# A mixture of 32 experts whose weights stream from HBM: pairs in a loop with a ring of 12 chunks, against experts unrolled with a ring of 21

## The chip, the cores and the metric

The kernel runs on one core of a Trainium2 chip. The metric is device time in microseconds (us). Five engines work side by side: PE (TensorE, matrix products), DVE (VectorE), ACT (ScalarE), POOL (GpSimd) and SP (SyncE, which here only issues transfers). They meet through semaphores. Sixteen DMA engines bring data from HBM to SBUF, the on-chip memory.

## What is computed

One encoder layer on 256 tokens of width 1024, all float32: a mixer (recurrence, attention, output product), then 32 experts, of which each token uses four, then a last norm. The change is in the experts and the last norm:

```
for e in range(N_EXPERTS):                         # 32
    gu = t @ w_gate_up[e] + b_gate_up[e]           # 1024 x 2048
    gate = minimum(gu[:, :1024], 7); up = clip(gu[:, 1024:], -7, 7)
    glu = gate * sigmoid(1.702 * gate)
    y = ((up + 1) * glu) @ w_down[e] + b_down[e]   # 1024 x 1024
    out = out + combine[:, e:e+1] * y
return rmsnorm(x + out, g_final)
```

## The kernel before

The mixer streams 40 chunks of 1 MB and ends at about 315 us. The experts follow. An expert's weights are 12 chunks of 1,048,576 bytes: eight of `w_gate_up` (a chunk is 128 rows, one row of 8 KB to each partition) and four of `w_down` (256 rows; each partition gets two rows of 4 KB that lie apart, `(i p) n`). All 32 experts are 384 chunks, 402.7 MB.

Only the tokens that chose an expert are worked on, up to 64 of them (`SLOTS`). For two experts at once (a pair) PE gathers their tokens by a product with a 0/1 matrix `sel` (`gather`, 16 matmuls into the PSUM banks `ga` and `gb`); ACT and DVE copy the result to `hg`. For each expert PE then runs `gate_up` (a bias product, then 8 chunks of 4 matmuls into `pj`), DVE and ACT form the activation in `prod`, PE turns it over (four transposes into `ga`), ACT copies it to `actT`, PE runs `down` (4 chunks of 4 matmuls into `gb`), ACT copies the result to `Y`, and PE adds it to the four output sums (`scatter`: 4 matmuls into `acc`, with the weighted selection `selWT`). PE does this in the written order, two experts in the body of a loop (`pair` in `Fori`, 15 passes after a first one written out). The matmuls of an fp32 product show in the trace as two records each, so an expert's `gate_up` is 64 records and its `down` 32.

SP issues one transfer for a chunk. A chunk of the ring of 12 is free when PE has finished the chunk that lay there (`chunk_done`). Before the experts start, 17 chunks are issued: the ring and five further buffers (`extra`) that are used only once. The mixer's `ring[0..7]` are the same bytes. SP's loads for expert 1 begin with chunk 3, since 0, 1, 2, 8 and 9 of it are already in the ring.

At the end DVE adds the residual `x_sb` to the four sums (`y_summed`), ACT squares and sums, and DVE scales and stores in two pieces.

## Time and profile before

| | |
|---|---|
| time, median of 3 runs | 1300.62 us (1297.96 to 1301.53) |
| span of the profiled execution | 1303.5 us |
| PE busy | 1167.4 us, 90% |
| DVE, ACT, POOL busy | 353.4, 265.5, 136.0 us |
| mean granted clock of TensorE | 0.964 |
| read from HBM | 448.19 MB |
| mixer | 0 to about 315 us |
| experts (first gate product to last down product) | 328.9 to 1292.2 us |

No time of the profiled execution is known apart from its span, so the span stands for it; it is 2.9 us above the median. "Busy" of PE counts each matmul from its start to a modelled end, with neighbours overlapping. A DMA share of 1.00 means that all 16 DMA engines had work all the time.

### The profile page before, as it was taken

Reading aid. Unit: us, or ns where it says so; the run is one execution under the profiler, and the core shown is the slowest. Engines: PE = TensorE matmul, PEld = TensorE weight load, DVE = VectorE, ACT = ScalarE, POOL = GpSimd, SP = SyncE. Lnnn points to the kernel's source line nnn. Section 1 sums busy time; section 2 is a strip of 40 time slices with the busy share of each in tenths; the row PEclk is TensorE's granted clock in tenths of the full one; section 3 lists DMA queues with packets and bytes.
Section 4 is the critical chain, followed back from the end, with each engine's and each line's share of the span. In section 5 each row is a group of like instructions: output and inputs, shape, how many; then the busy total and the mean of one; then the engine's idle time right before and its main releaser. Section 6 shows DMA issues by size and latency. Waiting matters only on the chain.

```text
span 1303.5 us, 16385 instructions
## 1 busy us (share of the span) xinstructions
PE 1167.4 (90%) x6418; PEld 613.3 (47%) x6418; DVE 353.4 (27%) x536; ACT 265.5 (20%) x378; POOL 136.0 (10%) x78
## 2 busy tenths in 40 slices
PE   4989999998998989898898989898989889898986
PEld 4988999988333333333333323332333323333322
DVE  5976888553111111111111111111111211111112
ACT  3536556534110101010101011010101010101102
POOL 5333333653000000000000000000000000000000
PEclk8989999998899989999999999999989999899999
DMA  9843444568499999999999999999999999999991
GB/s 251 259 140 122 158 131 146 169 210 352 182 386 417 409 409 410 418 418 418 418 418 415 417 416 417 417 417 418 418 418 418 418 418 418 418 416 417 417 417 48
DMA packets 118082, 449.75 MB, mean 345 GB/s; under 512 B 10416, under 2 KB 51456, under 8 KB 85280
## 3 DMA queue, kind: packets, MB, share of 16 engines
q1 hardware_dynamic: 117328, 447.04, 86.6%
q0 software_dynamic: 720, 2.23, 0.6%
q8 instruction: 24, 0.39, 0.1%
q14 instruction: 10, 0.08, 0.0%
HBM read 448.19 MB, written 1.05 MB: 345 GB/s over the span
## 4 chain that ended last, share of the span: by engine, by line
PE 85%; ACT 6%; DVE 5%; POOL 2%; issue 1%; DMA 1%; SPq 0%; DVEq 0%; ACTq 0%
PE pj L1155 34%; PE gb L1171 19%; PE pj L999 15%; PE s L1180 3%; PE ga L1133 3%; PE gb L1133 2%; PE pt L1180 2%; PE ga L1162 2%; PE pj L1150 2%; ACT mo L575 1%; ACT mo L573 1%; ACT w_hi L454 1%; POOL w_lo L386 1%; DVE GL L899 1%; DVE V L893 1%
## 5 line engine op out<-in xcount | busy, mean ns | idle before, releaser
L1155 PE MATMUL pj<-ring,GL 128*64 128x512 f32 x2024 | 441.3, 594 | 0.0
L1155 PEld LDWEIGHTS pj<-ring,GL 128*64 128x64 f32 x2024 | 142.6, 137 | 282.5 <-issue 282.5
L1171 PE MATMUL gb<-ring,mo 128*64 128x512 f32 x1008 | 242.4, 637 | 21.3 <-ACT mo L573 21.3
L889 DVE TENSOR_SCALAR V<-pj 128x512 f32<-128x512 f32 x32 | 22.1, 692 | 814.8 <-PE pj L1155 814.8
L1171 PEld LDWEIGHTS gb<-ring,mo 128*64 128x64 f32 x1008 | 74.2, 146 | 170.0 <-issue 140.8
L999 PE MATMUL pj<-hT_hi,w_hi 128*128 128x256 f32 x448 | 130.8, 292 | 15.0 <-DVE hT_lo L649 9.2
L386 POOL TENSOR_TENSOR w_lo<-ring,w_hi 128x1024 fp32r<-128x1024 f32 x40 | 113.3, 2833 | 170.3 <-ACT w_hi L454 170.3
L569 ACT ACTIVATE V<-V 128x512 f32<-128x512 f32 x32 | 20.1, 630 | 532.6 <-DVE V L889 532.6
L999 PE MATMUL pj<-hT_lo,w_hi 128*128 128x256 f32 x448 | 128.3, 286 | 0.0
L999 PE MATMUL pj<-hT_hi,w_lo 128*128 128x256 f32 x448 | 128.2, 286 | 0.0
L999 PEld LDWEIGHTS pj<-hT_hi,w_hi 128*128 128x128 f32 x448 | 87.4, 195 | 16.7 <-issue 16.5
L454 ACT ACTIVATE w_hi<-ring 128x2048 fp32r<-128x2048 f32 x40 | 76.4, 1910 | 86.7 <-PE pj L999 80.2
L999 PEld LDWEIGHTS pj<-hT_lo,w_hi 128*128 128x128 f32 x448 | 87.6, 196 | 0.2
L999 PEld LDWEIGHTS pj<-hT_hi,w_lo 128*128 128x128 f32 x448 | 87.5, 195 | 0.0
L644 DVE TENSOR_TENSOR w_lo<-ring,w_hi 128x1024 fp32r<-128x1024 f32 x40 | 66.8, 1669 | 55.1 <-ACT w_hi L454 51.9
L575 ACT ACTIVATE mo<-gb 128x512 f32<-128x512 f32 x32 | 19.1, 597 | 250.6 <-PE gb L1171 250.6
L1162 PE MATMUL ga<-ident,mo 128*128 128x128 f32 x128 | 23.3, 310 | 48.4 <-DVE mo L895 35.9
L1180 PE MATMUL s<-mo,GL 64*128 64x512 f32 x128 | 36.1, 641 | 22.3 <-ACT mo L575 22.3
L1162 PEld LDWEIGHTS ga<-ident,mo 128*128 128x128 f32 x128 | 14.9, 152 | 56.5 <-DVE mo L895 39.4
L1133 PEld LDWEIGHTS ga<-L,h 128*128 128x128 f32 x272 | 33.3, 200 | 14.4 <-issue 13.0
L1133 PE MATMUL ga<-L,h 128*128 128x128 f32 x272 | 36.6, 290 | 1.3 <-DVE L L869 1.3
L1180 PEld LDWEIGHTS s<-mo,GL 64*128 64x128 f32 x128 | 9.6, 184 | 50.5 <-ACT mo L575 50.5
(277 smaller groups left out, 1066.5 us busy)
## 6 DMA issues: line engine op xcount, KB each, us to landing
ring<-in_w_gate_up SPq DMA_DIRECT2D x253, 1024.0 KB, 10.6
ring<-in_w_down SPq DMA_DIRECT2D x126, 1024.0 KB, 9.6
ring<-in_w_in SPq DMA_DIRECT2D x28, 1024.0 KB, 6.3
ring<-in_w_lru_out SPq DMA_DIRECT2D x4, 1024.0 KB, 4.9
ring<-in_w_fox_out SPq DMA_DIRECT2D x4, 1024.0 KB, 5.6
ring<-in_w_o SPq DMA_DIRECT2D x4, 1024.0 KB, 4.9
extra<-in_w_gate_up SPq DMA_DIRECT2D x3, 1024.0 KB, 8.3
extra<-in_w_down SPq DMA_DIRECT2D x2, 1024.0 KB, 6.1
```

What stands on the lines that cost most here:

```text
L386: g.tensor_tensor(w_lo[c % 2][:, KT // 2:, :], src[:, KT // 2:, :], w_hi[c % 2][:, KT // 2:, :].bitcast(F32), ALU.subtract).then_inc(lo_po ...
L454: act.activation(w_hi[c % 2][:, :, :], ring[:, c % MIX_RING, :].rearrange("p (k n) -> p k n", k=KT), ACT.Identity).then_inc(hi_ready, 1)
L575: act.activation(Y, gb[:, :], ACT.Identity).then_inc(y_ready, 1)
L644: v.tensor_tensor(w_lo[c % 2][:, 0:KT // 2, :], src[:, 0:KT // 2, :], w_hi[c % 2][:, 0:KT // 2, :].bitcast(F32), ALU.subtract).then_inc(lo ...
L889: v.tensor_scalar(gate, pj[0][:, :], LIMIT, None, ALU.min).then_inc(gate_ready, 1)
L999: last = mm(pj[b][:, a * S:(a + 1) * S], lhs, rhs, start=(k == 0 and n == 0), stop=(k == KT - 1 and n == 2))
L1133: last = mm((ga, gb)[k // 4][:, k % 4 * P:(k % 4 + 1) * P], h2[:, t, k * P:(k + 1) * P], sel[:, t, :, 0:SLOTS], start=(t == 0), stop=(t == ...
L1150: mm(pj[b][:, :], onehot[:, i, :], bgu[:, b * 512:(b + 1) * 512], start=True, stop=False)
L1155: last = mm(pj[q // 2][h:h + SLOTS, :], hg[:, c, i, :], w[:, q * 512:(q + 1) * 512], start=False, stop=(c == GU_CHUNKS - 1))
L1162: last = nc.tensor.transpose(ga[:, j * P:(j + 1) * P], prod[:, j * P:(j + 1) * P], ident[:, :])
L1171: last = mm(gb[h:h + SLOTS, :], actT[:, f % 4, f // 4, :], w[:, a * D + q * 512:a * D + (q + 1) * 512], start=(f == 0), stop=(f == KT - 1))
L1180: last = mm(acc[t][q][:, :], selWT[h:h + SLOTS, i, t * P:(t + 1) * P], Y[h:h + SLOTS, :], start=False, stop=True, skip_group_check=True)
```

## The change

1. The 32 experts are written out on PE, ACT and DVE, and the 384 loads on SP; the loops are gone.
2. The weights go through 21 buffers (`slot`). The first 19 chunks, in order of use, go to buffers that come free during the mixer and the routing; two more (`LATE_SLOTS`: the bytes of `LG` and `x_sb`) come free when the output sums have been opened (`sums_open`). From chunk 19 on a load waits for the last user of its slot.
3. `w_down` is read as `(p i) n`: a partition gets two neighbouring rows, 8 KB that lie together. The transposes of the activation pick every second column to match.
4. On PE, the gather of the next pair is cut into halves, one behind each expert's `gate_up`; the scatter of expert n-1 stands behind `gate_up` of expert n, half ahead of the transposes of the activation and half behind them. The transposes write `pj` and not `ga`. `y_ready` is waited for an expert later.
5. The residual is added by PE when the sums are opened (four products with the identity, ACT's first sigmoid waits for them). The last norm reads the sums in PSUM: DVE's four additions go, ACT squares from PSUM into `junk` with a wait after each, all four squares before the first root, and DVE scales in four pieces of 512.
6. `sel` is 128x256 and not 128x512; `selW` is built in two operations. `bgu_raw` is loaded after the attention's last product and not after its last scores. `g_final` is loaded when slot 19 has had its last chunk (number 363 of 0 to 383).

The core of the diff (the loop over a pair in the overflow rounds, which these inputs don't enter, is left out):

```diff
-EXTRA = (0, 1, 2, 8, 9)
+FIRST_SLOTS, LATE_SLOTS = 19, 2
+N_SLOTS = FIRST_SLOTS + LATE_SLOTS
+CYCLE = (*range(GU_CHUNKS), *range(FIRST_SLOTS, N_SLOTS), *range(GU_CHUNKS, FIRST_SLOTS))
+SLOT_OF = [*range(FIRST_SLOTS)] + [CYCLE[q % N_SLOTS] for q in range(ALL_CHUNKS - FIRST_SLOTS)]
...
+        slot_at = [k_at, *mix_at[0:5], hl_at, mix_at[5], xc_at, lp_at, mix_at[6], mix_at[7], whi_at[0], wlo_at[0], r_at, i_at,
+                   whi_at[1], wlo_at[1], q_at, lg_at, x_at]
...
-                    src = w_down[bass.ds(e, 1), 2 * j * P:2 * (j + 1) * P, :].rearrange("e (i p) n -> p (e i) n", p=P)
-                    buf = buf.rearrange("p (i n) -> p i n", i=2)
+                    src = w_down[bass.ds(e, 1), 2 * j * P:2 * (j + 1) * P, :].rearrange("e (p i) n -> p (e i n)", i=2)
...
-            with sp.Fori(2, N_EXP) as e:
-                load_expert(e, e * EXP_CHUNKS + MIX_CHUNKS)
+            for q, s in enumerate(SLOT_OF):
+                if USER_BEFORE[q] is None:
+                    free_after[slot_at[s]]()
+                else:
+                    sp.wait_ge(chunk_done, MIX_CHUNKS + USER_BEFORE[q] + 1)
+                load_chunk(q // EXP_CHUNKS, q % EXP_CHUNKS, s)
...
-            g.wait_ge(chunk_done, MIX_CHUNKS + GU_CHUNKS)
+            g.wait_ge(chunk_done, MIX_CHUNKS + LAST_USER[LG_SLOT] + 1)
             g.dma_start(gfin_b, g_final.rearrange("(a n) -> a n", a=1).broadcast_to([P, D])).then_inc(gfin_loaded, 16)
...
+            act.wait_ge(sums_open, 1)
+            for n in range(N_EXP):
+                sigmoid_of(n)
+                if n % 2 and n + 1 < N_EXP:
+                    hg_copy(n // 2 + 1)
+                actT_copy(n)
+                if n % 2 == 0:
+                    if n:
+                        act.wait_ge(scattered, TT * n)
+                    selWT_copy(n // 2)
...
+                Y_copy(n)
...
+            act.wait_ge(gfin_loaded, 16)
             for t in range(TT):
+                act.wait_ge(scattered, TT * N_EXP - 1 + t)
                 for h in range(2):
-                    act.wait_ge(y_summed, 2 * t + h + 1)
-                    act.activation(h2[:, t, h * 512:(h + 1) * 512], yo[:, t, h * 512:(h + 1) * 512], ACT.Square,
+                    act.activation(junk, acc[t][h][:, :], ACT.Square,
                                    accum_out=stat[:, 40 + 2 * t + h:41 + 2 * t + h]).then_inc(sumsq3, 1)
+                    act.wait_ge(sumsq3, 2 * t + h + 1)
...
-            for t in range(TT):
-                dve.wait_ge(scattered, TT * N_EXP - 1 + t)
-                for h in range(2):
-                    v.tensor_tensor(yo[:, t, h * 512:(h + 1) * 512], x_sb[:, t, h * 512:(h + 1) * 512], acc[t][h][:, :],
-                                    ALU.add).then_inc(y_summed, 1)
...
+                        last = mm(acc[t][h][:, :], ident[:, :], x_sb[:, t, h * 512:(h + 1) * 512], start=False, stop=True,
+                                  skip_group_check=True)
+                last.then_inc(sums_open, 1)
...
+            for n in range(N_EXP):
+                p, i = divmod(n, 2)
...
+                gate_up(i, chunk_at)
+                if n == 0:
+                    open_sums()
+                if p + 1 < PAIRS:
+                    if i == 0:
+                        pe.wait_ge(sel_ready, p + 2)
+                    else:
+                        pe.wait_ge(y_ready, n)
+                    gather_half(i)
+                if i == 0:
+                    pe.wait_ge(selw_ready, p + 1)
+                    pe.wait_ge(up_ready, n + 1)
+                    transpose_selW()
+                if n:
+                    pe.wait_ge(y_ready, n)
+                    scatter(1 - i, 0)
+                pe.wait_ge(act_ready, n + 1)
+                transpose_act()
+                if n:
+                    scatter(1 - i, 1)
+                pe.wait_ge(actT_ready, n + 1)
+                if i == 1 and p + 1 < PAIRS:
+                    pe.wait_ge(hgb_ready, p + 2)
+                down(chunk_at)
```

First place, PE in the body of the loop, the first expert of a pair, from the last matmul of `gate_up` to the bias product of the next expert. `ring` holds weights, `PT` is the weighted selection, `mo` holds `prod`, `actT` and `Y`, `GL` holds `hg` and `selWT`:

```order
L1155 MATMUL pj1<-ring_49,GL_67 64x512 x2
L1200 MATMUL gb<-ident,PT 128x128 x4
L1160 REGISTER_ALU
L1162 MATMUL ga<-ident,mo_76 128x128 x4
L1171 MATMUL gb<-ring_49,mo_76 64x512 x8
L1143 REGISTER_ALU
L1171 MATMUL gb<-ring_49,mo_76 64x512 x8
L1180 MATMUL s0<-mo_76,GL_67 128x512
L1180 MATMUL s1<-mo_76,GL_67 128x512
L1180 MATMUL pt<-mo_76,GL_67 128x512
L1180 MATMUL po<-mo_76,GL_67 128x512
L1150 MATMUL pj0<-bgu_78,onehot_80 128x512
```

The same place in the changed kernel (expert 2). `V` holds the activation and `actT`, `Y` has a buffer of its own:

```order
L1166 MATMUL pj1<-slot10_93,GL_74 64x512 x2
L1155 MATMUL ga<-GL_74,h2_82 128x128 x8
L1173 MATMUL pj1<-ident,selW_108 128x128 x4
L1196 MATMUL s0<-Y_107,GL_74 128x512
L1196 MATMUL s1<-Y_107,GL_74 128x512
L1178 MATMUL pj0<-ident,V_73 128x128 x4
L1196 MATMUL pt<-Y_107,GL_74 128x512
L1196 MATMUL po<-Y_107,GL_74 128x512
L1189 MATMUL gb<-slot11_94,V_73 64x512 x4
L1189 MATMUL gb<-slot12_95,V_73 64x512 x4
L1189 MATMUL gb<-slot13_96,V_73 64x512 x4
L1189 MATMUL gb<-slot14_97,V_73 64x512 x4
```

Half a gather (L1155) and two halves of the scatter of the expert before (L1196) now stand around the transposes of the activation (L1178), and nothing stands between `down` and the next bias product.

Second place, SP's loads after the mixer's last chunk in the kernel before:

```order
L285 DMA ring_49<-in_w_gate_up 128x2048 x5
L285 DMA extra2_73<-in_w_gate_up 128x2048
L285 DMA ring_49<-in_w_gate_up 128x2048
L285 DMA extra0_71<-in_w_gate_up 128x2048
L285 DMA extra1_72<-in_w_gate_up 128x2048
L285 DMA ring_49<-in_w_gate_up 128x2048 x2
L285 DMA ring_49<-in_w_down 128x2x1024
L285 DMA extra8_74<-in_w_down 128x2x1024
L285 DMA ring_49<-in_w_down 128x2x1024
L285 DMA extra9_75<-in_w_down 128x2x1024
L285 DMA ring_49<-in_w_down 128x2x1024 x2
L285 DMA ring_49<-in_w_gate_up 128x2048 x5
```

In the changed kernel, from the last chunk that needs no chunk of an expert to be finished (number 18) on:

```order
L301 DMA slot18_101<-in_w_gate_up 128x2048
L301 DMA slot0_83<-in_w_gate_up 128x2048
L301 DMA slot1_84<-in_w_down 128x2048
L301 DMA slot2_85<-in_w_down 128x2048
L301 DMA slot3_86<-in_w_down 128x2048
L301 DMA slot4_87<-in_w_down 128x2048
L301 DMA slot5_88<-in_w_gate_up 128x2048
L301 DMA slot6_89<-in_w_gate_up 128x2048
L301 DMA slot7_90<-in_w_gate_up 128x2048
L301 DMA slot19_102<-in_w_gate_up 128x2048
L301 DMA slot20_103<-in_w_gate_up 128x2048
L301 DMA slot8_91<-in_w_gate_up 128x2048
```

Before, the eighteenth load waits for chunk 3 of expert 0. Now the twentieth (`slot0`) waits for chunk 0 of expert 0, the next seven for chunks 1 to 7, then two for `sums_open`. A load of `w_down` is one run of 2048 numbers to a partition and not two of 1024.

## Rows read from the trace of the kernel before

**Rows 1.** Windows: us, busy PE PEld DVE ACT POOL, granted clock, DMA share, GB/s.
```profile
325.00:337.00 12.00, 11.50 (x62) 5.48 (x63) 1.16 (x4) 2.13 (x3) 0.00 (x0) 0.98 0.05 11
...
352.00:357.00 5.00, 5.00 (x24) 1.64 (x22) 0.00 (x0) 0.00 (x0) 0.00 (x0) 0.93 0.00 2
...
366.00:1272.00 906.00, 816.88 (x3854) 311.19 (x3852) 115.04 (x180) 90.18 (x135) 0.00 (x0) 0.97 1.02 416
```
**Rows 2.** Waits of PE from 340 to 1280: waiter, releaser: us, times, longest.
```profile
PE ga L1162 <- DVE mo L895: 35.9, 15, 2.4
PE s L1180 <- ACT mo L575: 21.6, 31, 0.7
PE gb L1171 <- ACT mo L573: 21.3, 31, 0.7
PE ga L1162 <- DVE GL L899: 11.8, 15, 0.8
```
**Rows 3.** Timeline of SP's queue: start us, us, line, count.
```profile
335.97 7.20 SPq L285 DMA_DIRECT2D ring<-in_w_gate_up  x5
356.60 2.10 SPq L285 DMA_DIRECT2D ring<-in_w_down  x2
```
**Rows 4.** The chain that ended last, in order of time: start us, us.
```profile
328.91 13.88 PE pj L1155 x64
...
633.36 13.91 PE pj L1155 x64
...
652.02 9.34 PE gb L1171 x32
...
694.89 13.91 PE pj L1155 x64
...
753.74 13.91 PE pj L1155 x64
```
**Rows 5.** Timeline, between first and second product: start us, us, [idle before <- releaser].
```profile
708.71 0.66 PE L1200 MATMUL gb<-ident,PT 128*128 128x128 f32 x4
...
711.75 0.66 PE L1162 MATMUL ga<-ident,mo 128*128 128x128 f32 x4 [2.39 <-DVE mo L895]
...
713.10 7.09 PE L1171 MATMUL gb<-ring,mo 128*64 128x512 f32 x32 [0.69 <-ACT mo L573]
...
722.80 0.73 PE L1150 MATMUL pj<-bgu,onehot 128*128 128x512 f32 x2
...
737.34 2.05 PE L1133 MATMUL ga<-L,h 128*128 128x128 f32 x16
```
**Rows 6.** Timeline, opening of the four output sums.
```profile
343.31 1.98 PE L1125 MATMUL s<-LG,L 32*128 32x512 f32 x4
...
346.05 1.91 PE L1125 MATMUL po<-LG,L 32*128 32x512 f32 x2
```
**Rows 7.** Windows inside one pair of experts, columns as in rows 1.
```profile
703.00:719.00 16.00, 12.92 (x64) 4.63 (x62) 3.97 (x6) 1.71 (x3) 0.00 (x0) 1.00 1.01 423
721.00:729.00 8.00, 8.00 (x36) 2.79 (x38) 0.00 (x0) 0.00 (x0) 0.00 (x0) 1.00 1.03 410
```
**Rows 8.** DMA of the page, parts 3 and 6: queues, issues, us to landing.
```profile
q8 instruction: 24, 0.39, 0.1%
...
ring<-in_w_gate_up SPq DMA_DIRECT2D x253, 1024.0 KB, 10.6
```
**Rows 9.** Timeline of the end.
```profile
1292.26 0.60 ACT L575 ACTIVATE mo<-gb 128x512 f32<-128x512 f32 x1 [7.19 <-PE gb L1171]
...
1294.81 0.63 ACT L604 ACTIVATE h<-yo 128x512 f32<-128x512 f32 x1
...
1299.11 1.28 DVE L952 SCALAR_TENSOR_TENSOR yo<-yo,stat,extra 128x1024 f32<-128x1024 f32 x1
```
**Rows 10.** Windows around a clock drop, columns as in rows 1.
```profile
654.00:656.00 2.00, 2.00 (x6) 0.49 (x6) 0.00 (x0) 0.00 (x0) 0.00 (x0) 0.50 1.00 418
656.00:658.00 2.00, 2.00 (x10) 0.66 (x8) 0.00 (x0) 0.00 (x0) 0.00 (x0) 0.87 1.01 422
```

More of the change, by code:

```diff
@@ L195, in hybrid_block @@
         acc = [[ps[0], ps[1]], [pt, po]]
[L198 to L199 removed]
+        mix_loaded = [sem(f"mix{i}_loaded") for i in range(MIX_RING)]
+        loaded = [sem(f"slot{i}_loaded") for i in range(N_SLOTS)]
         x_loaded = [sem(f"x{t}_loaded") for t in range(TT)]
@@ new lines, in open_sums, with gather_half @@
+                        last = mm(acc[t][h][:, :], ident[:, :], x_sb[:, t, h * 512:(h + 1) * 512], start=False, stop=True,
+                                  skip_group_check=True)
+                last.then_inc(sums_open, 1)
+            def gather_half(b):
+                for k in range(b * KT // 2, (b + 1) * KT // 2):
+                    for t in range(TT):
+                        last = mm((ga, gb)[b][:, k % 4 * P:(k % 4 + 1) * P], h2[:, t, k * P:(k + 1) * P], sel[:, t, :, :],
+                                  start=(t == 0), stop=(t == TT - 1))
+                last.then_inc(gathered, 1)
@@ new lines, in gate_up @@
+            def gate_up(i, chunk_at):
+                for b in range(2):
+                    mm(pj[b][:, :], onehot[:, i, :], bgu[:, b * 512:(b + 1) * 512], start=True, stop=False)
+                for c in range(GU_CHUNKS):
+                    w = chunk_at(c)
+                    for q in range(4):
+                        h = SLOTS * (q % 2)
+                        last = mm(pj[q // 2][h:h + SLOTS, :], hg[:, c, i, :], w[:, q * 512:(q + 1) * 512],
+                                  start=False, stop=(c == GU_CHUNKS - 1))
+                    last.then_inc(chunk_done, 1)
@@ L1178, in scatter, with down @@
+            def down(chunk_at):
+                for c in range(DN_CHUNKS):
+                    w = chunk_at(GU_CHUNKS + c)
+                    for a in range(2):
+                        f = 2 * c + a
                         for q in range(2):
                             h = SLOTS * q
-                            last = mm(acc[t][q][:, :], selWT[h:h + SLOTS, i, t * P:(t + 1) * P], Y[h:h + SLOTS, :],
-                                      start=False, stop=True, skip_group_check=True)
-                        last.then_inc(scattered, 1)
@@ L1214, in expert_round, with scatter @@
-                if first:
-                    pair(0, True)
-                with pe.Fori(int(first), PAIRS) as p:
-                    pair(p)
-            expert_round(0, 0, 0, True)
+                            last = mm(gb[h:h + SLOTS, :], actT[:, f % 4, f // 4, :],
+                                      w[:, a * D + q * 512:a * D + (q + 1) * 512], start=(f == 0), stop=(f == KT - 1))
+                    last.then_inc(chunk_done, 1)
+            def scatter(i, t):
+                for q in range(2):
+                    h = SLOTS * q
+                    last = mm(acc[t][q][:, :], selWT[h:h + SLOTS, i, t * P:(t + 1) * P], Y[h:h + SLOTS, :],
+                              start=False, stop=True, skip_group_check=True)
+                last.then_inc(scattered, 1)
@@ L1220, in _, with chunk_at @@
             over = pe.value_load(flag_i[0:1, 0:1], min_val=0, max_val=1)
+            pe.wait_ge(y_ready, N_EXP)
+            for t in range(TT):
+                scatter(1, t)
             with pe.If(over > 0):
                 with pe.Fori(1, ROUNDS) as r:
-                    expert_round(r * (PAIRS + 1), r * N_EXP, r * PAIRS)
+                    with pe.Fori(0, PAIRS) as p:
+                        pair = r * PAIRS + p
+                        pe.wait_ge(sel_ready, pair + 1)
+                        gather_half(0)
+                        gather_half(1)
+                        pe.wait_ge(hga_ready, pair + 1)
+                        pe.wait_ge(hgb_ready, pair + 1)
+                        pe.wait_ge(onehot_ready, pair + 1)
+                        for i in range(2):
+                            n = r * N_EXP + p * 2 + i
+                            def chunk_at(c):
+                                pe.wait_ge(loaded[c], n * 16 + 16 * (SLOT_OF.count(c) - N_EXP + 1))
+                                return slot[c]
+                            gate_up(i, chunk_at)
+                            pe.wait_ge(act_ready, n + 1)
+                            if i == 0:
+                                pe.wait_ge(selw_ready, pair + 1)
+                                transpose_selW()
+                            transpose_act()
+                            pe.wait_ge(actT_ready, n + 1)
+                            pe.wait_ge(selwt_ready, pair + 1)
+                            down(chunk_at)
+                            pe.wait_ge(y_ready, n + 1)
+                            for t in range(TT):
+                                scatter(i, t)
```

439 lines of the change are left out of this document (204 added, 235 removed).

## The prediction

> **What bounds the kernel now.** I read the windows by stage first. From 366 to 1272 us the DMA engines have a share of 1.02 and move 416 GB/s [rows 1]: they never run dry. In the same stretch PE is busy 817 of 906 us, and the list of its waits names no transfer: it waits for DVE's activation (35.9 us in 15 times, once in a pair of experts) and for three kinds of copies (21.6, 21.3 and 11.8 us) [rows 2]. So two things run at almost one pace. PE takes 58.85 us for a pair of experts where the clock holds (694.89 to 753.74), and 61.53 where it drops (633.36 to 694.89, with a `down` of 9.34 us) [rows 4]. The transfers need 24 chunks of 1.0486 MB at 416 GB/s, 60.5 us. Every load waits for a chunk that PE has finished, so PE's clock still sets when loads start; but a PE that is faster alone gains little, since the transfers take over.
>
> The chunks are 384. The windows show two holes ahead of the steady part: 325 to 337 us at 11 GB/s and 352 to 357 us at 2 GB/s [rows 1]. SP's queue says why: the 18th chunk goes out at 335.97, after chunk 3 of expert 0, and behind the five of that burst the next two wait until 356.60 [rows 3]. The full stretch ends at 1272 us [rows 1], while PE's last `down` ends just ahead of ACT's copy at 1292.26 [rows 9]: PE is 20 us behind the transfers.
>
> **PE after the change.** Between the two products of an expert before, the transposes start at 711.75 where the product ended at 708.71, and `down` at 713.10 [rows 5]. Of this 4.39 us, 0.66 are the `selW` transposes, 0.66 those of the activation, 2.39 and 0.69 are idle. Now half a gather (2.05, from 737.34 [rows 5]), the `selW` transposes (0.66) and half a scatter (1.0: from the end of `down` at 720.19 to the bias product at 722.80 [rows 5] are 2.6 us, 0.7 of them idle [rows 2]) stand in the 3.04 us until the activation is ready: 3.7 us of work, no wait left. For the second expert it is 2.05 + 1.0 = 3.05 us, just enough. The other half of the scatter covers the 0.69 us of ACT's copy, and `Y` is wanted an expert later, so the 0.7 us ahead of each scatter go too. Idle time in a pair is 35.9/15 + 11.8/15 + 2 x 21.6/31 + 2 x 21.3/31 = 5.9 us [rows 2]. PE's own work is then 58.85 - 5.9 = 53.0 us a pair, 26.5 an expert.
>
> The transfers need 29.9 us an expert (below). PE catches up 3.4 us an expert on a lead of some 19 chunks (48 us), so about half-way, near expert 13, it starts to wait for weights. From there on what PE saves is worth nothing. **The end is set by the transfers**, and the gain is what they gain: an earlier restart, a better rate, and PE's lag of 20 us at the end.
>
> **Start of the transfers.** The mixer and the routing are unchanged but for small things: `sel` is half as wide, `selW` takes two operations, both beside PE. I cost them at 0 (-0.5 to +1). `bgu_raw` comes later but is not wanted before ACT's part at the third output chunk. So gate products start at 328.9 as before [rows 4]. A chunk of them takes 13.88/8 = 1.74 us, so load 19 is issued at 330.7. Data follow an issue by about 0.9 us (issued 335.97, window until 337 nearly empty [rows 1, 3]): 331.6. 19 chunks are in or under way, 365 are left.
>
> **Rate.** A window in which mainly `w_gate_up` lands moves 423 GB/s, one with `w_down` 410 [rows 7]. This stands in the place where the four `down` loads, issued some 10 us earlier, must land. The only difference is the row: 8 KB against two of 4 KB. A chunk takes 2.48 us at 423 and 2.56 at 410. Weighted 2 to 1 this is 2.507, and the steady part gives 1.0486/0.416 = 2.52, a factor 1.005. With `w_down` in 8 KB rows I take 2.48 x 1.005 = 2.493 for all. 365 of them are 910 us. Bounds: no gain, 365 x 2.52 = 920; or the 2.48 without the factor, 905.
>
> The Trainium skill ("DMA: Bandwidth & Descriptors", Why small descriptors are slow) charges a fixed 3 or so cycles for each packet of 32-byte beats, so 3/131 on 4 KB and 3/259 on 8 KB. By that a `down` chunk would gain 1.1% and not 3%, 3.5 us in all, and the time would be 6 us more than mine; the rows of this trace, with 3%, decide.
>
> **Holes that are left.** Eight loads (19 to 26) follow PE's first gate chunks, 20 us of transfers, until 351.5. Loads 27 and 28 wait for `sums_open`. PE ends the gate product at 342.8 and opens the sums: four bias products took from 343.31 to 347.96 [rows 6], and four products with the identity are new; at the same price that is 9.3 us, until 352. Then come data for 5 us. Load 29 wants the first `down` chunk, behind half a gather, the `selW` transposes, ACT's sigmoid (which waits for the sums) and the transposes: about 359.5. I count 3.5 us of holes (0 to 8). `g_final`, 0.52 MB, now loads in the full stretch: 1.3 us. The written-out code is some 1.7 times as long by the instructions in order; the instruction queue moved 0.39 MB for all of it [rows 8], so 0.3 MB more, 0.7 us. The last byte is at 331.6 + 910 + 3.5 + 1.3 + 0.7 = 1247; I add 1 for the semaphore: 1248. All other waits of SP are older than its queue is long and cost nothing.
>
> **Tail.** PE then has one chunk of `down`, a quarter of 7.1 us, 1.8: 1249.8. Before, from there (1292.2) to the end it was 11.3 us. Now ACT's `Y` (0.60), half the scatter and the squares: the first square started 2.6 us after the product [rows 9], and so again. Four squares with a wait after each are 4 x 0.9 = 3.6 (0.63 and the read of the sum). Then DVE's sum, root and reciprocal 0.7, two scalings of 0.68, the same chain for the second half 0.6 and 1.37, then the store, 3.1 as before (1300.4 to 1303.5): 13.4 us. That is 2.1 us worse than before; the bounds are +0.5 and +3. I add 0.5 for a slow clock in the last chunk (0 to 4).
>
> **Sum.** 1249.8 + 13.4 + 0.5 = 1263.7 us of span, against 1303.5: -39.8. The parts: PE's lag at the end -17.5 (20.3 to 2.8), the restart 5 us earlier, two more chunks ahead and the second hole together -18, the rate -9, against +2 for `g_final` and code and +2.6 for tail and clock. The profiled execution is 2.9 above the median, so the time is 1260.8, rounded **1261**.
>
> **Rivals.**
> *The rate stays* at 416 (the 410 comes from the place in the pair, not from the rows). For it: the low windows also fall on the time in which PE starts a product. Against it: they fall equally behind both experts' `down`. Time 1261 + 10 = 1271. Chance 0.15.
>
> *PE stays the bound.* If the fillers don't cover (a copy is late, ACT's order holds the transposes), PE keeps up to its 58.85 us a pair. From 328.9 with 9 us of opening and 16 pairs of 57 to 58.85 it ends `down` at 1250 to 1279.5, and the time is 1272 to 1290. Against: 3.7 us of work in 3.04. The Trainium skill ("TensorE: Matmul & The Clock Gate", HAM oscillation) warns that waits for loads between matmuls put TensorE back to its slow clock, and this PE waits 0.75 us a chunk once it has caught up. The rows show the fall to 1.2 GHz (0.50) after idle time, and the return within 656 to 658 under continuous work [rows 10]; such a fall cost 9.34 - 7.11 = 2.2 us in a `down`. A PE that falls behind finds its chunks loaded and works without a gap, which brings the clock back; so I expect it to follow the transfers within a few us. Only if half of its work were slow would it be the bound. Chance 0.10, all of it here.
>
> *Slower than before: code.* The loop's code was fetched once; now PE runs through about one 16 KB block (0.39 MB in 24 [rows 8]) an expert, beside transfers whose queue is full. If a block is asked for only when it is wanted, it lands like a chunk, after 10.6 us [rows 8]: 37 us an expert, 32 of them end at 1525, time about 1535. It makes the kernel slower where an expert takes PE over 29.8 us on average ((1291 - 337)/32), so from a stop of 3.3 us a block. Against: all but a few of the 24 blocks are the mixer's straight code, and their whole share of the DMA engines is 0.1%; for it: only in the expert stage is the queue full. Chance 0.04.
>
> *The change doesn't do what it says*: the 21 slots give no deeper lead, since loads queue in one line. That is true and without price: a full queue is all that is wanted. It is part of the forecast.
>
> **How the numbers follow.** The forecast has 0.69, with its own range 1254 to 1268: the rate bounds -5 and +10, the holes -3.5 and +4.5, the tail and clock -2 and +4, not all at once. The rest (0.02) is a change that comes to nothing. The range to hold 8 in 10 takes in the unchanged rate and the beginning of a bound PE: 1253 to 1277. This kernel's runs tell 0.3% (3.9 us) from no change. Faster: 0.69 + 0.15 + 0.10 = 0.94. Same 0.02, slower 0.04.
>
> **What the profile will show.** DMA share about 1.0 from 332 us to about 1247 without the two holes, but for one to four us near 352 to 360; GB/s 421 or so and flat, with no dips to 410 (if they stay, the rate step is wrong). PE's idle time in the first pairs nearly zero, 53 us a pair; from about expert 13 on PE waits for transfers, 59.8 us a pair. If the pairs take 57 or more from the start and no transfer is waited for, the filler step is wrong. The last `down` ends 2 to 3 us after the last byte. The squares to the store take 13 us. If PE stops for several us at no semaphore in the expert stage, the code rival holds.

## The result and the profile after

The changed kernel takes **1269.7 us** (median of 4 runs, 1267.5 to 1272.4) against 1301.0 us for the kernel before beside it (4 runs, 1298.0 to 1301.5). The ratio is 0.9766, 95% interval 0.974 to 0.979: faster by 2.3%. The forecast was 1261, its range 1253 to 1277; the time lies in that range, but above the narrower 1254 to 1268 that the prediction gave for its own mechanism. The profiled execution took 1272.4 us with a span of 1270.6.

The windows answer to [rows 1] and [rows 7]; their columns are the same.

```profile
325.00:332.00 7.00, 6.34 (x37) 5.31 (x38) 2.24 (x8) 0.97 (x2) 0.00 (x0) 0.77 0.42 174
332.00:345.00 13.00, 13.00 (x62) 4.20 (x58) 0.00 (x0) 0.00 (x0) 0.00 (x0) 1.00 0.82 328
352.00:357.00 5.00, 4.62 (x28) 3.18 (x26) 1.38 (x2) 0.88 (x2) 0.00 (x0) 1.00 0.93 342
366.00:1244.00 878.00, 828.64 (x3882) 300.13 (x3880) 110.22 (x194) 70.96 (x120) 0.60 (x1) 1.00 1.01 421
703.00:719.00 16.00, 15.99 (x81) 6.47 (x79) 4.70 (x9) 2.31 (x4) 0.00 (x0) 1.00 1.01 421
721.00:729.00 8.00, 6.55 (x28) 1.46 (x24) 0.00 (x0) 0.00 (x0) 0.00 (x0) 1.00 1.01 421
```

From 366 to 1244 us the DMA engines stay full and move 421 GB/s, where it was 416. The two small windows differed before, 423 and 410; now both show 421. The second hole, 352 to 357 us at 2 GB/s, is nearly filled, and the granted clock from 366 to 1244 us is 1.00 (it was 0.97).

PE's waits, as in [rows 2]:

```profile
PE pj L1166 <- DMA slot<-in_w_gate_up: 46.6, 84, 1.3
PE pj L1178 <- DVE V L915: 2.0, 1, 2.0
PE pj L1173 <- DVE V L909: 1.5, 1, 1.5
...
```

The regular waits for DVE and ACT, 90.6 us in [rows 2], are gone but for one of each at the first or the last expert. In their place stand 84 waits for gate chunks. In the first pairs there is none; PE goes from one product to the next. This is the timeline of a pair, from the even expert's gate product on:

```profile
391.50 13.95 PE L1166 MATMUL pj<-slot,GL 128*64 128x512 f32 x64
405.39 2.05 PE L1155 MATMUL ga<-GL,h 128*128 128x128 f32 x16
...
407.81 1.13 PE L1196 MATMUL s<-Y,GL 64*128 64x512 f32 x4
...
410.60 7.09 PE L1189 MATMUL gb<-slot,V 128*64 128x512 f32 x32
...
418.28 13.96 PE L1166 MATMUL pj<-slot,GL 128*64 128x512 f32 x64
...
444.69 1.51 PE L1166 MATMUL pj<-slot,GL 128*64 128x512 f32 x6
```

444.69 less 391.50 is 53.2 us a pair, where it was 58.85 or 61.53 [rows 4]. Once PE has caught up, the same stretch looks like this (the timeline near 700 us; in brackets the idle time ahead and what ended it):

```profile
701.97 1.94 PE L1166 MATMUL pj<-slot,GL 128*64 128x512 f32 x8 [0.55 <-DMA slot<-in_w_gate_up]
...
761.63 1.94 PE L1166 MATMUL pj<-slot,GL 128*64 128x512 f32 x8 [0.56 <-DMA slot<-in_w_gate_up]
```

Both are an odd expert's last gate chunk: 59.66 us a pair, 24 chunks at 2.49. PE does a chunk in 1.94 and waits 0.55. The first such wait in the trace is at 664.7 us, in expert 12.

At the end the transfers don't stop at once. The chain of waits shows what stands behind the last gate chunk:

```profile
1243.17 1.96 PE pj L1166 x8
...
1245.16 0.70 DVE V L908
...
1248.16 0.74 PE pj L1178 x4
...
1250.01 8.64 PE gb L1189 x32
...
1266.11 0.75 DVE x_sb L973
```

The windows there are 0.90 full (1244 to 1246 us), then 0.63, 0.49, 0.40 and 0.01. Before it was a sharp edge, 0.92 and then 0.11. The landings of single loads tell more. Each load of 1 MB signals 16 times, once from each DMA engine; I took first and last of the 16 from the trace's semaphore events. In the kernel before they lie 0.5 to 2.5 us apart, from 520 us on 1.6 to 2.2. In the changed one they are 2.6 us apart near 400 us, and the distance grows in steps of some 1.5 us to 7.5 us at the end. The last load lands first at 1245.5 and last at 1253.0. The chain shows the same steps. From one last gate chunk to the next it takes 29.82 us, and 31.4 us where a step falls in between:

```profile
1031.56 1.96 PE pj L1166 x8
...
1062.93 1.96 PE pj L1166 x8
...
1092.75 1.88 PE pj L1166 x7
```

The page's instruction queue moved more, too, against [rows 8]:

```profile
q8 instruction: 52, 0.85, 0.3%
...
slot<-in_w_gate_up SPq DMA_DIRECT2D x256, 1024.0 KB, 27.0
```

### The profile page after: what moved, and what is told of

It reads as the page before. It is cut to its first block, busy times and chain, and to the rows that moved or that the text cites. A ratio compares the mean times of both kernels' runs of the same rounds, so it can differ in the third digit from the quotient of the medians.

```text
span 1270.6 us, 14720 instructions
## 1 busy us (share of the span) xinstructions
PE 1172.3 (92%) x6394; PEld 598.8 (47%) x6394; DVE 344.2 (27%) x546; ACT 245.7 (19%) x362; POOL 138.1 (11%) x78
## 4 chain that ended last, share of the span: by engine, by line
PE 47%; DMA 44%; ACT 2%; DVE 2%; POOL 2%; issue 1%; SPq 1%; DVEq 0%; ACTq 0%
DMA slot<-in_w_gate_up 43%; PE pj L1166 16%; PE pj L1020 15%; PE gb L1189 7%; PE ga L1155 1%; ACT w_hi L452 1%; POOL w_lo L385 1%; PE gb L1155 1%; PE pt L1196 1%; PE s L1196 1%; SPq L301 1%; DMA mix<-in_w_in 1%; PE pj L1178 1%; PE pj L1161 1%; PE s L1062 1%
## 5 line engine op out<-in xcount | busy, mean ns | idle before, releaser
L1166 PE MATMUL pj<-slot,GL 128*64 128x512 f32 x2048 | 467.3, 599 | 47.8 <-DMA slot<-in_w_gate_up 46.6
L1166 PEld LDWEIGHTS pj<-slot,GL 128*64 128x64 f32 x2048 | 135.4, 136 | 363.1 <-issue 223.7
L1189 PE MATMUL gb<-slot,V 128*64 128x512 f32 x1024 | 228.4, 599 | 0.7 <-ACT V L570 0.7
L1189 PEld LDWEIGHTS gb<-slot,V 128*64 128x64 f32 x1024 | 71.1, 138 | 153.5 <-issue 129.1
L385 POOL TENSOR_TENSOR w_lo<-mix,w_hi 128x1024 fp32r<-128x1024 f32 x40 | 115.1, 2879 | 170.3 <-ACT w_hi L452 170.3
L452 ACT ACTIVATE w_hi<-mix 128x2048 fp32r<-128x2048 f32 x40 | 76.3, 1909 | 88.3 <-PE pj L1020 81.8
L662 DVE TENSOR_TENSOR w_lo<-mix,w_hi 128x1024 fp32r<-128x1024 f32 x40 | 66.8, 1669 | 57.9 <-ACT w_hi L452 53.8
L1155 PEld LDWEIGHTS ga<-GL,h 128*128 128x128 f32 x256 | 31.5, 200 | 13.0 <-issue 11.8
L1196 PE MATMUL s<-Y,GL 64*128 64x512 f32 x128 | 36.1, 641 | 0.7 <-ACT Y L578 0.7
L1155 PEld LDWEIGHTS gb<-GL,h 128*128 128x128 f32 x256 | 30.3, 195 | 12.2 <-issue 12.2
L1196 PE MATMUL po<-Y,GL 64*128 64x512 f32 x64 | 35.9, 640 | 0.0
L1196 PE MATMUL pt<-Y,GL 64*128 64x512 f32 x64 | 35.9, 640 | 0.0
```

The costliest lines, as they stand in the source:

```text
L385: g.tensor_tensor(w_lo[c % 2][:, KT // 2:, :], src[:, KT // 2:, :], w_hi[c % 2][:, KT // 2:, :].bitcast(F32), ALU.subtract).then_inc(lo_po ...
L452: act.activation(w_hi[c % 2][:, :, :], mix[c % MIX_RING].rearrange("p (k n) -> p k n", k=KT), ACT.Identity).then_inc(hi_ready, 1)
L662: v.tensor_tensor(w_lo[c % 2][:, 0:KT // 2, :], src[:, 0:KT // 2, :], w_hi[c % 2][:, 0:KT // 2, :].bitcast(F32), ALU.subtract).then_inc(lo ...
L1155: last = mm((ga, gb)[b][:, k % 4 * P:(k % 4 + 1) * P], h2[:, t, k * P:(k + 1) * P], sel[:, t, :, :], start=(t == 0), stop=(t == TT - 1))
L1166: last = mm(pj[q // 2][h:h + SLOTS, :], hg[:, c, i, :], w[:, q * 512:(q + 1) * 512], start=False, stop=(c == GU_CHUNKS - 1))
L1189: last = mm(gb[h:h + SLOTS, :], actT[:, f % 4, f // 4, :], w[:, a * D + q * 512:a * D + (q + 1) * 512], start=(f == 0), stop=(f == KT - 1))
```

## The experiments

They were timed in three groups, each in turns with the kernel before, whose medians there were 1303.8, 1304.1 and 1303.8 us. Ratios are to those runs. The changed kernel itself was timed again in the last group; it comes first here.

**The changed kernel again.**

> The changed kernel itself, unchanged, on the chip and beside the runs that the next kernels are compared with. If the differences so far are to be read as they stand, its ratio to before is 0.975 to 0.978.

Measured: 1270.6 us (1268.1 to 1272.0, 6 runs), ratio 0.9766 (0.973 to 0.980). Ratios of other kernels are read against this one. The intervals are wide because the kernel before scatters (1292 to 1307 us); the changed kernels' own runs lie within 2 to 7 us, and where two of them don't overlap I go by medians.

**w_down in 4 KB rows again.**

```
-  src = w_down[e, 2*j*P : 2*(j+1)*P, :] "e (p i) n -> p (e i n)"
+  src = ... "e (i p) n -> p (e i) n";  dst = slot "p (i n) -> p i n"
-  transposes of up "p (b r i) -> p b i r" [:, j//2, j%2, :]
+  transposes of up[:, j*P:(j+1)*P]
```

> The changed kernel, but w_down is read in two rows of 4 KB for each partition as before, with the transposes of the activation taking its columns in order. Theory (the rows set the rate): 128 chunks take 2.56 us in place of 2.49, the transfers end 9 us later and the time is 1279 (1276 to 1281); in the stretch 600 to 1200 us the rate is 416 to 417 GB/s in place of 421, and windows of a few us around the down loads show 410. Rival (the low rate of before came from the place in the pair, not from the rows): 1270, 421 GB/s. By the Trainium skill's fixed cost of a packet (DMA: Bandwidth & Descriptors, Why small descriptors are slow) it would be 3.5 us more, 1273.

Measured: 1278.5 us (1276.3 to 1279.8), ratio 0.9828 (0.979 to 0.987), 8 us more than the changed kernel. The windows over one pair:

```profile
700.00:709.00 9.00, 7.83 (x44) 3.73 (x44) 3.49 (x6) 1.19 (x3) 0.00 (x0) 1.00 1.02 410
709.00:718.00 9.00, 9.00 (x40) 2.81 (x42) 1.21 (x4) 1.12 (x2) 0.00 (x0) 1.00 1.03 423
...
727.00:736.00 9.00, 7.31 (x35) 2.23 (x31) 0.66 (x2) 0.00 (x0) 0.00 (x0) 1.00 1.01 410
736.00:745.00 9.00, 9.00 (x50) 4.13 (x50) 2.02 (x4) 1.82 (x3) 0.00 (x0) 1.00 1.03 419
```

The dips to 410 GB/s are back and the mean over 600 to 1200 us is 417 in place of 421. So the rate depends on the rows, not on the place in the pair: this decides against the rival *the rate stays*. The 3.5 us, an estimate from the packet cost in the Trainium skill ("DMA: Bandwidth & Descriptors", Why small descriptors are slow), are too little.

**w_down in 8 KB rows, in the kernel before.**

```
-  "e (i p) n -> p (e i) n", buf "p (i n) -> p i n";  transposes of prod[:, j*P:(j+1)*P]
+  "e (p i) n -> p (e i n)";  transposes of prod "p (b r i) -> p b i r" [:, j//2, j%2, :]
```

> The kernel before, with w_down read in one row of 8 KB for each partition and the transposes taking the product's columns in that order; nothing else. Theory (in the kernel before PE sets the end, 20 us behind the transfers): the faster transfers only make the queue shallower or the lag of PE longer; 0 to -4 us, 1297 to 1301, with PE's pairs at 58.9 where the clock holds. Rival (the transfers paced that kernel as well): the whole 9 us, 1292.

Measured: 1304.1 us, ratio 1.0014 (0.999 to 1.004): no change. The same edit is worth 8 us in the changed kernel and nothing here, because here PE is the later one: its pace decides when a load is issued. The transfers only end earlier ahead of it, the last landing at 1269.2 us where the trace of the kernel before has 1273.5, while PE's waits stay, 87.7 us in all for 89.2.

**PE's order undone, the rest kept.**

```
   gate_up(i)
-  gather_half(i) ... scatter(1-i, 0); transpose_act; scatter(1-i, 1); down
+  [i == 1: gather_half(0); gather_half(1)]; wait act; transpose_act; down
+  wait y_ready(n + 1); scatter(i, 0); scatter(i, 1)
```

> The changed kernel with its 21 slots, 8 KB rows, identity products and written-out code, but PE's order as before: both halves of the gather behind the second expert's gate product, the whole scatter behind its own down product with the wait for Y ahead of it. Theory (PE's waits keep it at 58.9 us or more a pair, close to the transfers' 59.7, so that it ends behind them): no filler means no catching up of the lag; down ends at 331 + 10 + 16 x (58.9 to 59.7), 1283 to 1296 less nothing, and the time is 1283 to 1298, 13 to 28 us more. Rival (the transfers are the bound either way, and the gain came from ring and rows): 1270 to 1274, at most 4 us more, from the last chunks alone.

Measured: 1330.7 us (1329.0 to 1332.4), ratio 1.023 (1.019 to 1.027): slower than the kernel before, and 33 us above the top of what I had expected. Its timeline:

```profile
694.37 7.09 PE L1189 MATMUL gb<-slot,V 128*64 128x512 f32 x32 [0.69 <-ACT V L570]
...
720.17 0.63 PE L1173 MATMUL pj<-ident,selW 128*128 128x128 f32 x4 [1.48 <-DVE V L909]
721.74 0.74 PE L1178 MATMUL pj<-ident,V 128*128 128x128 f32 x4 [0.94 <-DVE V L915]
723.71 9.95 PE L1189 MATMUL gb<-slot,V 128*64 128x512 f32 x32 [1.22 <-ACT V L570]
```

One `down` in each pair takes 9.95 us for 7.09. Pairs take 61.4 us (29.2 and 32.2). The slow `down` comes in every pair; the kernel before had one of 8.8 to 9.3 us in ten of 15 pairs. Without the fillers nothing of the gain is left.

This isn't quite the order of the kernel before. The `selW` transposes write `pj` here and so wait for DVE (1.48 us); before they wrote `gb` and didn't wait. Idle time in a pair is nearly the same, 85.1/15 = 5.7 us for 5.9, but it stands in more pieces. The waits alone don't say when the clock falls, either. In the kernel before the same two waits that [rows 5] shows ahead of a `down` of 7.09 us stand ahead of a slow one a pair earlier:

```profile
650.22 1.11 PE L1162 MATMUL ga<-ident,mo 128*128 128x128 f32 x4 [2.39 <-DVE mo L895]
...
652.02 9.31 PE L1171 MATMUL gb<-ring,mo 128*64 128x512 f32 x32 [0.69 <-ACT mo L573]
```

**Only the scatter undone.**

```
-  if n: wait y_ready(n); scatter(1-i, 0)   ...   if n: scatter(1-i, 1)
   down
+  wait y_ready(n + 1); scatter(i, 0); scatter(i, 1)
```

> The changed kernel with the halves of the gather as fillers, but the scatter undone: it stands whole behind its own down product with the wait for Y. Idle time a pair of experts is then 0.3 + 1.0 + 2 x 0.69 + 2 x 0.70 = 4.1 us on 53.2 of work, 57.3 us, under the transfers' 59.7. Theory 1 (fillers count only until PE is faster than the transfers): the end is set by the transfers as in the changed kernel, 0 to 5 us more, ratio 0.977 to 0.980. Theory 2 (as the kernel with nothing filled showed, where every even expert's down product ran at 9.9 in place of 7.1 us behind waits of 1.5, 0.9 and 1.2 us: what costs is the clock that falls behind clustered waits): if the clock falls here as well, 60.2 us a pair, over the transfers' pace, and the time is near 1315, ratio 1.01; if it holds, as Theory 1.

Measured: 1327.4 us (1323.1 to 1329.7), ratio 1.0187 (1.016 to 1.022). As in Theory 2, all of it is back with the scatter's filler gone, and 12 us more than that theory's 1315, since the clock falls behind both experts' waits and not behind one. The timeline, and the windows around its `down`:

```profile
721.27 0.74 PE L1178 MATMUL pj<-ident,V 128*128 128x128 f32 x4 [0.63 <-DVE V L915]
723.24 8.78 PE L1189 MATMUL gb<-slot,V 128*64 128x512 f32 x32 [1.22 <-ACT V L570]
...
753.72 8.78 PE L1189 MATMUL gb<-slot,V 128*64 128x512 f32 x32 [0.69 <-ACT V L570]
```

```profile
721.00:723.00 2.00, 0.74 (x4) 0.55 (x4) 0.22 (x1) 0.94 (x2) 0.00 (x0) 1.00 1.06 442
723.00:726.00 3.00, 2.76 (x8) 1.12 (x10) 0.00 (x0) 0.14 (x1) 0.00 (x0) 0.57 0.97 407
726.00:728.00 2.00, 2.00 (x10) 0.68 (x7) 0.00 (x0) 0.00 (x0) 0.00 (x0) 0.79 1.10 442
```

In windows of 1 us the granted clock is 0.50, that is 1.2 GHz, from shortly after the start of `down` at 723.2, and 1.00 again from 727. This happens behind both experts' waits. A pair has 5.0 us of waits (74.5 in 15 pairs) and 2 x 1.7 of slow clock: 53.2 + 5.0 + 3.4 = 61.6 us; the trace has 61.5. That is over the transfers' 59.7, so PE ends everything.

**Only the gather undone.**

```
-  if p + 1 < PAIRS: gather_half(i)
+  if i == 1 and p + 1 < PAIRS: gather_half(0); gather_half(1)
```

> The changed kernel with the scatter halves as fillers, but the gather undone: both halves stand behind the second expert's gate product. The first expert keeps a wait of 1.5 us ahead of the selW transposes; the rest is covered but for 0.1 to 0.7 us. Theory (what made the two kernels with the scatter undone slower than before is the clock, which falls when several waits follow one another around the activation, 0.6 + 1.2 or 1.1 + 0.7 us): here one wait of 1.5 us stands alone, the clock holds, a pair takes 55 to 56 us of PE, under the transfers' 59.7, and the time is as the changed kernel's, 0 to 3 us more. Rival (the order of PE as a whole must be as in the change, or the clock falls): 1.2 to 2.9 us a down product more, 58 to 61 us a pair, 1280 to 1320.

Measured: 1270.9 us (1269.5 to 1271.4), ratio 0.9765 (0.973 to 0.980): as the changed kernel.

```profile
PE pj L1166 <- DMA slot<-in_w_gate_up: 32.5, 59, 1.7
PE pj L1173 <- DVE V L909: 22.2, 15, 1.5
PE pj L1178 <- DVE V L915: 2.0, 1, 2.0
```

A wait of 1.5 us in every pair costs nothing. `down` stays at 7.09 us behind it; PE catches up a little later and waits less often for weights (32.5 us in place of 46.6). So it isn't the idle time as such but where it leads: PE must be under 59.7 us a pair, the slow clock included. What exactly makes the clock fall the runs don't settle. Behind one wait of 1.5 us with full work around it, it held; behind 1.5, 0.9 and 1.2 us, behind 0.6 and 1.2, and behind 1.1 and 0.7, it fell in every pair; behind 2.4 and 0.7, in the kernel before, in ten of 15.

No run has the new order of PE in the kernel before, and none has the loops with the new ring. So what order and ring are worth each for itself isn't measured.

**PE without the transfers' brake.**

```
+  if c >= GU_CHUNKS and e >= 2:
+      src = w_down[e, 2*j*P : 2*(j+1)*P : 2, :];  dma_start(slot[s][:, 0:D], src)
```

This kernel doesn't compute the layer. From expert 2 on it leaves out every second row of `w_down`, 30 x 4 x 0.524 = 63 MB (the expectation's 31 MB is half of that), and the products take what the slot held.

> The changed kernel, but from expert 2 on only half of each w_down chunk is loaded (every second row of it, 0.5 MB in rows of 4 KB); the products use what the rest of the slot holds. It leaves out 31 MB of 403. Theory (PE's own work is 53.2 us a pair, and the clock stays up because no wait is left): an expert's transfers take 25 us, less than PE's 26.6, so PE never waits for weights: 331 + 34 + 30.5 x 26.6 = 1176 for the last down product's end, 1190 in all. Rival (PE keeps pace only because the transfers hold it back, and with no slack left it meets late copies or the slow clock): 28 to 29.4 us an expert, 1220 to 1262.

Measured: 1200.1 us (1199.5 to 1202.8), ratio 0.9227 (0.919 to 0.926). PE never waits for a weight, and its windows are full at full clock:

```profile
600.00:800.00 200.00, 199.97 (x962) 76.28 (x960) 24.79 (x43) 17.23 (x29) 0.00 (x0) 1.00 0.99 394
800.00:1000.00 200.00, 199.97 (x968) 77.57 (x966) 29.49 (x52) 18.34 (x31) 0.00 (x0) 1.00 1.00 396
```

The pace is the expected one (26.8 and 26.4 us an expert). My total of 1190 was wrong by counting half an expert too few: 330 + 34 + 30 x 26.6 + 26 for the last expert is 1188, and that is where its `down` ends. With 16 landings 1.9 us apart at the end, the drift doesn't show here either, although the code is the same: PE holds the loads back, and the engines that are late catch up.

**More code.**

```
+  for n in range(30):
+      for _ in range(192): g.wait_ge(chunk_done, MIX_CHUNKS + n * EXP_CHUNKS + 1)
```

> The changed kernel with 192 more wait instructions for each of 30 experts on the idle POOL (all on a semaphore that is reached anyway): 5760 instructions of code that must be fetched beside the full queue. Theory (each fetched block sets one DMA engine's share of the loads back, as the spread of a load's 16 landings in the changed kernel suggests: it grows from 2.6 to 7.5 us in jumps of 1.55 us for every eight of PE's blocks): 2 to 8 us more, 1272 to 1278, the last loads' landings spread over more than 7.5 us. Rival (code costs only its bytes, 0.37 MB more): 0.9 us, 1270.6. Rival 2 (the jumps have nothing to do with code): no change, 1270, spread 7.5 us.

Measured: 1277.2 us (1275.3 to 1279.3), ratio 0.9819 (0.978 to 0.986): 6.6 us more. The added code came in 22 blocks of 8 KB (the queue q14, 0.12 MB, is at 0.30):

```profile
q14 instruction: 37, 0.30, 0.1%
```

```profile
1240.00:1244.00 4.00, 3.29 (x16) 0.67 (x12) 0.00 (x0) 0.00 (x0) 0.00 (x0) 1.00 1.01 420
1244.00:1248.00 4.00, 3.09 (x14) 0.97 (x16) 0.00 (x0) 0.00 (x0) 0.00 (x0) 1.00 0.71 297
1248.00:1252.00 4.00, 3.46 (x16) 0.79 (x12) 0.69 (x2) 0.00 (x0) 0.00 (x0) 1.00 0.33 137
...
1256.00:1260.00 4.00, 4.00 (x14) 1.16 (x14) 0.00 (x0) 0.00 (x0) 0.00 (x0) 0.66 0.04 16
```

The bulk of the engines is done as early as before, near 1244 us. A few are late, and a chunk is complete only with its last sixteenth. The 16 landings are 15.1 us apart at the end (7.5 in the changed kernel), and the last gate chunk comes at 1249.3 in place of 1243.2. 0.18 MB at 421 GB/s would be 0.4 us. So a block costs the engine that fetches it far more than its bytes, and that engine sets the time of every load. What the blocks do that the kernel fetches anyway can be read from the times of the fetches in the traces. In the changed kernel 16 KB blocks were fetched at 575.0, 802.4 and 1042.2 us, and the landings move apart by 1.5 us at 577.7, 805.4 and 1045.5. Eight profiled executions have the transfers as the bound and no code added. In them the distance grows by more than 0.3 us 47 times between 400 and 1200 us, each time 2.1 to 4.2 us behind the fetch of a block. The largest 14 of these steps, 1.0 to 1.7 us, stand eight 16 KB blocks apart within an execution.

**A ring of 19.**

```
-FIRST_SLOTS, LATE_SLOTS = 19, 2
+FIRST_SLOTS, LATE_SLOTS = 19, 0
```

> The changed kernel without the two late slots (those that the opened sums free): a ring of 19. Theory (the number of chunks ahead counts only until the steady part): two chunks fewer are loaded before the first down chunk is done, a hole of about 5 us near 352 to 359, and nothing else, since a queue of 19 is full as well: 5 us more, ratio 0.9805. Rival (depth pays throughout, for example because it lets the DMA engines drift apart): more than 8 us. Rival 2 (PE catches up anyway, so nothing is lost): under 1 us.

Measured: 1275.1 us (1273.6 to 1276.0), ratio 0.9787 (0.976 to 0.982), 4.5 us above the changed kernel's median. The stretch 345 to 366 us moves 296 GB/s in place of 371, which is 3.7 us of transfers; from 366 us on it is 421 as with 21. Two slots are worth two chunks, once.

**The last two experts in another order.**

```
+ORDER[LAST*12:] = [gates of 30][gates of 31][down chunks of 30][down chunks of 31]
   n == 30:  ... actT copy;  gate_up(31);  down(30)
   n == 31:  scatter(30); transposes; down(31)
```

> The changed kernel with the last two experts' chunks loaded and used in another order: the gate chunks of expert 31 go ahead of the down chunks of expert 30, so the last eight loads are down chunks and the activation of expert 31 is made while expert 30's down product runs. Theory (at the end of the changed kernel 4.8 us of activation and all four down products, 8.7 us, stand behind the last gate chunk, 1243.2 to 1258.6, while the last byte lands near 1252.5): only one chunk's product is left behind the last byte, down ends at 1254.3, 4.3 us earlier; 0.34% of the time, ratio to before 0.973 in place of 0.9766. Rival (the drifted DMA engine's last share, not PE's order, sets the end of down, or PE falls to the slow clock while it waits for each down chunk): 0 to 1 us.

Measured: 1269.1 us (1268.5 to 1269.6), ratio 0.9743 (0.972 to 0.977): 1.4 us under the changed kernel's median, inside the scatter. In the trace `down` ends 2.7 us behind the last landing (1255.8 and 1253.1), in the changed kernel 5.6. But 1.6 of those 5.6 are the slow clock of that execution's last `down` (8.68 in place of 7.09 us), so that the edit gained 1.3. What was still in the way: `Y`, the scatter and the transposes, and then a whole `down`, stood behind expert 30's last chunk.

**The root of the first half early.**

```
   square(0,0); square(0,1); square(1,0)
+  root(0)
   square(1,1); root(1)      # junk buffer in two halves
```

> The changed kernel with another order on ScalarE in the last norm: the root of rows 0 to 127 directly behind their two squares and the next half's first one, two halves of the junk buffer in turn, so that a square doesn't wait for the one before it in its half. Theory (the last stage is a chain over ScalarE's four squares of 0.72 us and VectorE's four scalings of 0.68 us, end to end): the scalings of the first half run beside the squares of the second, 1.2 to 1.6 us less, ratio to before 0.9755. Rival (reading the same PSUM banks at the same time, or the waits, eat it up): 0 to 0.5 us.

Measured: 1269.4 us (1266.2 to 1272.7), ratio 0.9749 (0.972 to 0.978): as such not told apart. From the end of `down` to the end it takes 10.9 us, for 12.0.

**Both, and the end of PE's work rearranged.**

```
   down(30) chunks 0, 1;  transpose_act(31) -> actT_last;  down(30) chunks 2, 3
   down(31) chunk 0 -> ga;  scatter(30);  down(31) chunks 1, 2, 3 -> ga
```

> The changed kernel with three edits at its end. The last two experts' down chunks are loaded and used behind both experts' gate chunks; the last activation is transposed between down chunks of expert 30 into a buffer of its own, and expert 31's down product goes into a free bank, so that it follows expert 30's without a stop, the scatter of expert 30 standing between two of its chunks; and ScalarE's roots are moved up. Theory (the reordering alone gained only some 1.3 us, because Y, the scatter and the transposes of expert 30 and the whole down product of expert 31, 10.6 us, still stood behind the last chunk of expert 30): now one chunk's product is left behind the last landing; down ends 2 us behind it in place of 3.9, and the root gains the 1.1 us measured: 3 us less than the changed kernel, ratio 0.974. Rival (the slow clock or the drifted engine takes it back): under 1 us.

Measured: **1265.0 us** (1263.2 to 1267.4, 6 runs), ratio 0.9727 (0.969 to 0.976). Against 1270.6 (1268.1 to 1272.0) for the changed kernel in the same group that is 5.5 us less, and no run of one lies within those of the other. The timeline of its end:

```profile
1238.90 1.94 PE L1210 MATMUL gb<-slot,V 128*64 128x512 f32 x8 [0.53 <-DMA slot<-in_w_down]
1240.88 0.60 ACT L584 ACTIVATE Y<-gb 128x512 f32<-128x512 f32 x1 [3.75 <-PE gb L1210]
1241.42 1.94 PE L1210 MATMUL ga<-slot,GL 128*64 128x512 f32 x8 [0.58 <-DMA slot<-in_w_down]
...
1245.20 5.44 PE L1210 MATMUL ga<-slot,GL 128*64 128x512 f32 x24
1250.74 0.60 ACT L584 ACTIVATE Y<-ga 128x512 f32<-128x512 f32 x1 [9.27 <-PE ga L1210]
```

`down` ends 2.0 us behind the last landing (1250.7 and 1248.7). Of the 6.5 us between the two profiled spans (1268.0 and 1261.5), 3.6 are this (the changed kernel's `down` ended 5.6 us behind the last landing here too, 0.7 of them a slow clock), 1.1 the root; the other 1.8 are an earlier last landing (1250.4 there), of which 0.6 is an earlier start of the gate products. That part is scatter as far as I can tell.

## Why the prediction was right, and where its sum was off

The mechanism was right: PE stops being the one that is late, the transfers set the end. The time came out 8.9 us above the forecast, in its range. By the number alone the rival *the rate stays*, with 1271, was the nearer one; what decides for the forecast's mechanism is the rate of 421 GB/s and the experiment with 4 KB rows. In the span it is 1270.6 against 1263.7, and the steps are these.

- *PE's work, 53.0 us a pair; catching up near expert 13.* Right: 53.2, and the first wait for a weight is at 664.7 us, in expert 12.
- *The rate, 2.493 us a chunk.* Right: 421 GB/s is 2.49, and the experiment with 4 KB rows gives 8 us for the 9 counted. By the Trainium skill ("DMA: Bandwidth & Descriptors", Why small descriptors are slow) it would have been 3.5, an estimate; the runs decide for the rows of the trace. `g_final` cost the 1.3 us counted: the chain's interval in which it is loaded (issued at 1204.4) is 31.1 us for 29.8.
- *Start and holes.* The gate products started at 331.3, 2.4 us later than counted: the mixer's part was 2.1 us longer already at 225 us, and 1.6 of them arose in its first 34 us (the first load took 9.96 for 9.28 us, the first product 8.67 for 7.77), where no step of the change explains it. The second profiled execution of the same kernel started them at about 328, so this is how single executions differ. The holes were 2.6 us, for 3.5.
- *The code, 0.7 us.* **Mis-sized.** I counted bytes (0.3 MB; it was 0.46). The spread of landings says 7.5 less the 1.9 or so of before, some 5.6 us, and the experiment with more code moves spread (7.6 us more) and time (6.6 us more) together. Start, holes and code give 1248 + 2.4 - 0.9 + 4.9 = 1254.4; the last landing is at 1253.0. The chunks between the steps, at 29.82/12 = 2.485 us and not 2.493, would take 2.9 us off that, to 1251.5. So these terms close to about 1.5 us, not better. The rival with code had named the right resource, but the wrong price: it has PE stand still for a block, and no wait or stop of that kind is in the list of its waits.
- *"PE then has one chunk of down, 1.8."* **The step that failed.** The last gate chunk must be followed by the activation (4.8 us, of them 1.99 idle) and then by all four chunks of `down`, 7.1 us. No chunk is waited for in it: the last one has landed at 1253.0, before its quarter of `down` is due. I had treated `down` as if it followed the transfers chunk by chunk, and had forgotten the dependence ahead of it. Counted from the last landing, `down` ended after 5.6 us in place of 1.8; 1.6 of the difference is a slow clock (8.68). The kernel with the rearranged end has this step as I predicted it, 2.0 us; of the 5.5 us that it takes less, some 3 are this step.
- *Tail 13.4.* It was 12.0: the four squares stand 0.72 us apart, not 0.9, and the first starts 2.1 us behind `down`, not 2.6.
- *The profiled execution is 2.9 us above the median.* I took the span of before less 2.9 for the time. For the changed kernel the median is only 0.9 under the span; this makes the remaining 2 us.

In all: +5.0 at the last landing (the sum had 1248 with its semaphore), +3.8 from there to the end of `down`, -1.4 in the tail, -0.5 for the clock that I had counted apart, 6.9 in the span; and 2 from span to time.

The rival *the rate stays* is refuted by the 4 KB experiment. *PE stays the bound* is refuted as well, but it was much closer than its price says. I gave it 1272 to 1290 us, with PE at its old 58.85. With the scatter's filler gone the time is 1327: the clock falls in every pair. The waits of 0.55 us a chunk that this PE has now, on which the rival leaned, didn't lower it: the granted clock from 600 to 1200 us is 1.00. The *slower* rival did not occur.

## What to carry to other kernels

- Where two engines run at nearly one pace, an edit on either is worth only what it makes the later one gain: 8 KB rows gave 8 us with PE ahead and 0 with PE behind. And idle time that is under the limit on paper can go over it with the clock: 5.0 us of waits in a pair cost 3.4 more, where the kernel before paid 1.3 on average for 5.9.
- For the end of a stream, write down what depends on the last piece of each kind, not only on the last byte; loading what others wait for first, and giving the last product a bank and buffer of its own, took some 3 us off here.
- Code that is written out is fetched beside the data. It costs little by its bytes and more by delaying one of sixteen engines, all of which a load needs.

## What the runs showed of the hardware

- **DMA engines drift apart when nothing stops them.** With a full queue that waits for no one, each engine works through its own sixteenths. What delays one (here instruction blocks) adds up over the run, from 2.6 to 7.5 us in the changed kernel (8.0 in its second profiled execution) and to 15.1 with 22 more blocks. Where PE paces the loads, it stays at or under 2.5, 3.5 and 3.9 us (the kernel before, PE's order undone, half of `w_down`). That instruction blocks are what delays them is shown for added blocks. For the kernel's own blocks it rests on the times: all 47 steps over 0.3 us in eight executions stand 2.1 to 4.2 us behind the fetch of a block. No run took code away.
- **Rows of 4 KB and 8 KB differ by 3%**, 410 and 421 to 423 GB/s, at a full queue of loads of 1 MB.
- **The granted clock** went to 0.50 at the start of a product behind two or three waits of 0.6 to 1.5 us in a row, in every pair of experts. The product took 1.7 us more there behind two waits (8.78 for 7.09) and 2.9 behind three (9.95). Behind two waits of 2.4 and 0.7 us it fell in ten of 15 pairs. It did not fall once in 84 regular waits of 0.55 us, nor behind single ones of 1.5 us. Behind the single wait of 1.99 us ahead of the last `down` it fell in five of the eight traces that have it (8.68 us in the changed kernel), and held in three (7.09). What it depends on stays open.
